# Sliding attention: probability-value products of both heads of a pair in one step, even and odd head in turn

## The chip, the core and the metric

The kernel runs on one core of a Trainium2 chip. The metric is the device time of one execution in microseconds (us). Its engines are TensorE (PE, with its weight loads shown apart as PEld), VectorE (DVE), ScalarE (ACT), GpSimd (POOL) and SyncE (SP); each works through its own program in order, and they wait for each other on semaphores.

## What is computed

One layer of a hybrid decoder, over 2048 tokens with a model width of 1024. The change touches the sliding-window attention in its first part:

```python
h = h + W_out [ HGRN2 head group (4 heads) || sliding-window GQA head group (8 q heads) ](RMSNorm(h))
h = h + CrossAttn_4heads(RMSNorm(h), RMSNorm(mem))
h = h + W_down relu(W_up RMSNorm(h))^2

# swa_group: SW_HEADS = 8, SW_KV_HEADS = 2, SW_HEAD_DIM = 64, SW_BLOCK = WINDOW = 128
s = einsum('bnqhgd,bnkhd->bnhgqk', qb, kw) * 64 ** -0.5     # query block n, key blocks n-1 and n
s = where(valid, s, -inf)
m = maximum(max(s), sink);  p = exp(s - m)
denom = sum(p) + exp(sink - m)
o = einsum('bnhgqk,bnkhd->bnqhgd', p / denom, vw)           # the products that the change touches
```

Everything is float32. The queries of heads 0 to 3 share one head of keys and values, and those of heads 4 to 7 the other.

## The kernel before

The program has three parts in a row: the mixer (both head groups and the projections in front of them), the cross attention and the MLP. The mixer works on four blocks of 512 tokens, and every engine runs the same list of steps for a block. `mixer_steps` writes this list (MIX_STEPS); the last block has its own, LAST_STEPS, made from it, in which a first product of the cross attention (`cross_make`, parts 0 to 2) stands in places that the next block's work left empty. Three sources are interleaved by `weave` at places counted (PLACES): `hg`, the work of a recurrent head; `attend`, the attention of one pair of heads; and `panels`, the projections. A projection ("make") comes in three parts: parts 0 and 1 have eight matmuls each (L1560, L1563), part 2 has eight with the weights' low halves (L1570), all 128 rows by 512 columns. A block runs recurrent head 0, then four times a stretch with the attention of pair t = 0 to 3 (heads 2t and 2t+1) and behind it recurrent head t+1 (behind pair 3 the next block follows). Beside pair t the gates of head t+1 are made, and beside recurrent head 3 the next block's normed input is split (`norm_split`: ACT line 1096, DVE line 1314).

A pair of heads has four sub-steps q = 0 to 3, numbered a = 4t + q: q % 2 says whether the even or the odd head, q // 2 which two of the block's four query tiles of 128. Each sub-step goes through these steps:

- scores: PE (L1702) multiplies queries and keys into one of three banks of PSUM; DVE (L1502) adds mask and scale and takes the extreme of each row; ACT (L1244, L1248) takes the exponentials.
- scale: DVE adds the denominator, inverts it and multiplies the probabilities by it (L1514, L1516, and twice L1519).
- turn: PE transposes the four tiles of 128 by 128 (L1713) into the one bank TURN, and ACT (L1256) copies this bank to pT[a % 2]. PE waits for the copy of a-1 before it writes the bank; ACT waits for the products of a-2 before it writes pT[a % 2].
- pv: PE multiplies (L1725): four matmuls in float32, of which each stands as two records with their weight loads in the trace. The weights are a tile of values with 64 columns, and the products fill rows 0 to 63 of the bank OUT for the even head, rows 64 to 127 for the odd one.

After the fourth pv ACT copies OUT (L1262, step att_out). Then `hg_transpose` follows: PE transposes values (L1612) and decayed keys kend (L1617), and ACT copies both (L1211, and L1214 into ktok), which the products of L1625 (`hg_delta`) need. The scores of a recurrent head (L1642) come in steps of two halves: seven products into rows 0 to 63 of a bank, then seven into rows 64 to 127; the seventh of either half reads hq. The ends of kend and qdec are copied by ACT (L1192, L1193) and scaled by DVE (L1404, L1406) in the step `spans_end`. The output gate (`out_gate`) goes from ACT (L1199) to DVE (L1411) and back (L1202, L1204). A projection's result is taken by ACT (`take`; for queries L1148 and L1149, two activations of 128 by 512).

`attend` yields a group of steps for each n = 0 to 6, and `weave` counts these groups. On PE the steps from the second transposition of pair 1 on read turn, pv, part 2 of a make, turn, pv, turn, pv, pv, and the transpositions of the next recurrent head.

Of the kernel before, what the change touches and what calls it, by code (L numbers as in the profile page):

```python
# [26 lines left out]
P = 128  # L27
# [7 lines left out]
QT = TB // P  # L35
# [7 lines left out]
SW_D = 64  # L43
# [110 lines left out]
def mixer_steps():  # L154


    def rotated(n):
        return [[("sw_norm", n)], [("sw_root", n)], [("sw_rotate", n)]]

    def hg(h, beside):  # L160


        norm, root, rotate = rotated(beside)
        gates = [[("gate_start", h + 1)], [("gate_forget", h + 1)]]
        out = [[("out_gate", h)], [("out_gate_end", h)]]
        yield [("hg_transpose", h)]
        yield [("hg_scores", h, 0)]
        yield [("hg_scores", h, 1)]
        yield [("hg_delta", h)]
        yield norm  # L170
        yield [("hg_state", h)]
        yield [("hg_scores", h, 2)]
        yield root
        yield [("hg_o", h, 0)]
        yield from [out[0]] if h == 0 else [gates[0]] if h + 1 < HEADS else []
        yield [("hg_scores", h, 3)]
        yield [("hg_o", h, 1)]
        yield rotate
        yield from [out[1]] if h == 0 else [gates[0]] if h + 1 == HEADS else []
        yield [("hg_o", h, 2)]  # L180
        yield gates[1] if h else gates[0]
        yield [("hg_o", h, 3)]
        yield [("hg_square", h)]
        yield from [gates[1]] if h == 0 else []

    def hg_tail(h):
        return [[("hg_total", h)], [("hg_end", h)]]

    def attend(t):
        yield []  # L190
        for n in range(QT + 3):
            if n < QT:
                yield [("scores", t * QT + n)]
            if 0 <= n - 1 < QT:
                yield [("scale", t * QT + n - 1)] + [("turn", t * QT + n - 2)] * (n > 1)
            if n == QT + 1:
                yield [("turn", t * QT + n - 2)]
            if n >= 3:
                yield [("pv", t * QT + n - 3)]
        yield [("att_out", t)]  # L200

    def with_out_gate(steps, h):
        steps = list(steps)
        last = steps.index([("turn", h * QT - 1)])
        return steps[:last + 1] + [[("out_gate", h)]] + steps[last + 1:] + [[("out_gate_end", h)]]

    def each(kind):
        return [[(kind, k)] for k in range(KT)]

    yield from weave(hg(0, 0), panels(("sw_v", 0), ("sw_q", 0), ("hg_f", 1)), PLACES["head 0"])  # L210
    yield from weave([[("sw_values",)]] + hg_tail(0) + [[("sw_keys",)]] + rotated(1),
                     panels(("hg_q", 1)), PLACES["keys"])
    for h in range(1, HEADS + 1):
        attention = weave(attend(h - 1), hg_tail(h - 1) if h > 1 else [], PLACES["tail"])
        attention = weave(attention, panels(("hg_v", h), ("hg_g", h), ("sw_q", h) if h < NEXT else ("sw_k", h)), PLACES["pair"])
        attention = weave(attention, gates(h)[2:], PLACES["gates"])
        if h < HEADS:
            attention = with_out_gate(attention, h)
        yield from weave(attention, [[("norm_root", 0)]] if h == 2 else [], PLACES["root"])
        if h + 1 < HEADS:  # L220
            head = weave(hg(h, h + 1), panels(("hg_f", h + 1), ("hg_q", h + 1)), PLACES["head"])
            if h == 1:
                yield from weave(head, each("norm_square"), PLACES["squares"])
            else:
                yield from weave(head, each("norm_apply"), PLACES["apply"])
        elif h < HEADS:
            yield from weave(hg(h, h + 1), each("norm_split") + list(panels(("hg_f", NEXT), ("hg_q", NEXT))), PLACES["head 3"])
# [530 lines left out]
def mixer(nc, block, sems, sh, xT, w_mix, rope_d, y_d, w_cross, lows_d):  # L758
# [13 lines left out]
    OUT = bank[5]  # L772
# [3 lines left out]
    with ExitStack() as ctx:  # L776
# [49 lines left out]
        vsw = sb("vsw", [P, 1 + QT, P])  # L826
        s_sb = sb("s_sb", [P, 3, 2, 2 * P])
        pT = sb("pT", [P, 2, TB])
# [81 lines left out]
        a_pt = signal("probabilities_copied", NA)  # L910
        a_o = signal("attention_output_ready", NA)
# [618 lines left out]
        def _(pe):  # L1530
# [65 lines left out]
            def turn(blk, steps):  # L1596
                for step in steps:
# [70 lines left out]
                    elif kind == "sw_norm":  # L1668
                        n = step[1]
                        pe.wait_ge(copied.sem, copied.at(blk, panel_at("sw_q", n - 1) if n else panel_at("sw_k", 0)))  # L1670
                        if n == 0:
                            total(blk, step, c("ones64"), hsq[:, n % 2, :])
                        else:
                            tile_totals(blk, step, hsq[:, n % 2, :])
                    elif kind == "sw_rotate":
                        n = step[1]
                        if n == 1:
                            pe.wait_ge(k_ok1.sem, k_ok1.at(blk, 0))
                        else:
                            pe.wait_ge(st_ok.sem, st_ok.at(blk, max(n, 1) * (NCH + 1) - 1))  # L1680
                        if n == 0:
                            pe.wait_ge(s_tn.sem, s_tn.at(blk, 0))
                        else:
                            pe.wait_ge(copied.sem, copied.at(blk, panel_at("sw_q", n - 1)))
                        pe.matmul(ROT[:], rotq[:] if n else c("rot"), tn[:, n % 2, :], start=True, stop=True).then_inc(s_rot.sem, 1)
                    elif kind == "sw_keys":
                        pe.wait_ge(s_qk.sem, s_qk.at(blk, 0))
                        pe.wait_ge(v_ok.sem, v_ok.at(blk, 0))
                        pe.matmul(TURN[:], c("dup0"), tcos[:], start=True, stop=True).then_inc(k_dup0.sem, 1)
                        pe.matmul(ROT[:], c("dup1"), tcos[:], start=True, stop=True).then_inc(k_dup1.sem, 1)  # L1690
                    elif kind == "scores":
                        a = step[1]
                        t, q = ATT[a]
                        if q == 0:

                            pe.wait_ge(h_pr.sem, h_pr.at(blk, (t + 1) * NCH // 2 - 1))
                            pe.wait_ge(s_qk.sem, s_qk.at(blk, 1 + t))
                        if q >= 3:
                            pe.wait_ge(a_s.sem, a_s.at(blk, a - 3))
                        for i in range(2):  # L1700
                            tq = q // 2 * 2 + i
                            last = pe.matmul(SCORE[a % 3][:, i * 2 * P:(i + 1) * 2 * P],  # L1702
                                             qk[:, t % 2, tq * P:(tq + 1) * P],
                                             kpad[:, t // 2 * 2 + q % 2, tq * P:(tq + 2) * P], start=True, stop=True)
                        last.then_inc(a_sc.sem, 1)
                    elif kind == "turn":
                        a = step[1]
                        pe.wait_ge(a_pn.sem, a_pn.at(blk, a))
                        if ATT[a][1]:
                            pe.wait_ge(a_pt.sem, a_pt.at(blk, a - 1))  # L1710
                        for kt in range(2):
                            for i in range(2):
                                last = pe.transpose(TURN[:, (2 * kt + i) * P:(2 * kt + i + 1) * P],  # L1713
                                                    s_sb[:, a % 3, i, kt * P:(kt + 1) * P], c("ident"))
                        last.then_inc(a_tr.sem, 1)
                    elif kind == "pv":
                        a = step[1]
                        t, q = ATT[a]
                        if q == 0:
                            pe.wait_ge(h_y.sem, h_y.at(blk, t))  # L1720
                        pe.wait_ge(a_pt.sem, a_pt.at(blk, a))
                        for i in range(2):
                            tq = q // 2 * 2 + i
                            for kt in range(2):
                                last = pe.matmul(OUT[q % 2 * SW_D:(q % 2 + 1) * SW_D, tq * P:(tq + 1) * P],  # L1725
                                                 vsw[:, tq + kt, t // 2 * SW_D:(t // 2 + 1) * SW_D],
                                                 pT[:, a % 2, (2 * kt + i) * P:(2 * kt + i + 1) * P],
                                                 start=kt == 0, stop=kt == 1)
                        last.then_inc(a_o.sem, 1)

            pe.wait_ge(s_xhi, KT)
            pe.wait_ge(s_xln, 4 + KT)
# [1606 lines left out]
```

## Time and profile before

| | us |
|---|---|
| median of 3 runs | 2718.79 |
| lowest, highest | 2718.01, 2720.99 |
| span of the profiled execution | 2717.5 |
| mixer in it, about | 70 to 1012 |
| PE busy in the mixer | 907.6 of 942 |

In the profile a group of instructions is named by its line, its engine, and the tiles that it writes and reads. A matmul's record goes on until its result is out, so records of one step overlap: how fast PE goes is read from the starts, not from the durations. The timeline shows consecutive instructions of a line merged, with the start of the first, the time to the end of the last, and their number.

### The profile page before, as it was taken

The page shows a single profiled execution, that of the slowest core. Times are in us where ns is not written, and L with a number is a line of the kernel's source. Part 1 is how long each engine was busy: PE and PEld are TensorE (multiplying, and loading weights), DVE is VectorE, ACT ScalarE, POOL GpSimd, SP SyncE. Part 2 cuts the span into 40 slices and gives each one's busy share as a digit, 9 for nine tenths or more (in the row PEclk, how much of TensorE's full clock was granted, in tenths as well). Part 3 has the DMA queues.
Part 4 walks back from the last instruction along what each step waited for, and adds up shares of the span by engine and source line. Part 5 has one row for each costly group of instructions (what it writes and reads, how often), then busy time and mean ns, then how long its engine had stood idle before and what let it go on. Part 6 is the DMA issues. An engine that isn't in the chain of part 4 may idle for free.

```text
span 2717.5 us, 39324 instructions
## 1 busy us (share of the span) xinstructions
PE 2635.4 (97%) x13654; PEld 2160.8 (80%) x13654; DVE 1730.3 (64%) x3010; ACT 1146.5 (42%) x2179; POOL 895.6 (33%) x1018
## 2 busy tenths in 40 slices
PE   7999999999999999999999899999999999999999
PEld 5778778777877878777787788888888888888887
DVE  6677566756755665656657486787667354556665
ACT  4455454545544454654565322252223223322231
POOL 1332200000000017436534576747667222222223
PEclk9999999999999999999999999999999999999999
DMA  4422422243243234226315234423333963445664
GB/s 179 140 102 88 171 96 94 94 166 109 86 169 105 86 126 184 70 97 252 116 55 190 85 129 151 138 99 124 105 132 124 328 184 105 134 135 149 202 183 150
DMA packets 184509, 369.17 MB, mean 136 GB/s; under 512 B 13168, under 2 KB 79088, under 8 KB 181616
## 3 DMA queue, kind: packets, MB, share of 16 engines
q1 hardware_dynamic: 179152, 357.08, 39.1%
q10 hardware_dynamic: 5152, 9.51, 1.0%
q8 instruction: 110, 1.80, 0.3%
q14 instruction: 95, 0.78, 0.1%
HBM read 286.71 MB, written 79.82 MB: 135 GB/s over the span
## 4 chain that ended last, share of the span: by engine, by line
PE 76%; DVE 9%; issue 5%; ACT 4%; POOL 3%; DMA 2%; ACTq 0%; DVEq 0%; SPq 0%; POOLq 0%
PE bank L3255 7%; PE bank L3253 7%; PE bank L3257 7%; PE bank L1570 5%; PE bank L3233 5%; PE bank L1560 5%; PE bank L3229 5%; PE bank L3230 5%; PE bank L1563 5%; PE bank L1642 3%; PE bank L2183 2%; PE bank L2178 2%; PE bank L2179 2%; PE bank L1725 2%; PE bank L1702 2%
## 5 line engine op out<-in xcount | busy, mean ns | idle before, releaser
L478 POOL TENSOR_TENSOR wlo<-raw,whi 128x256 fp32r<-128x256 f32 x372 | 320.5, 894 | 1151.5 <-ACT whi L1162 667.5
L1560 PE MATMUL bank<-hi,whi 128*128 128x512 f32 x704 | 296.3, 421 | 2.1 <-ACT whi L1158 1.9
L1563 PE MATMUL bank<-lo,whi 128*128 128x512 f32 x704 | 278.0, 395 | 5.9 <-DVE lo L1314 5.9
L3257 PE MATMUL bank<-hi,wlo 128*128 128x512 f32 x896 | 275.8, 389 | 0.0
L3253 PE MATMUL bank<-hi,whi 128*128 128x512 f32 x896 | 275.8, 389 | 0.0
L3255 PE MATMUL bank<-lo,whi 128*128 128x512 f32 x896 | 275.8, 389 | 0.0
L3045 DVE TENSOR_TENSOR lo<-h,hi 128x1024 fp32r<-128x1024 f32 x80 | 124.6, 1557 | 172.8 <-ACT hi L2809 172.8
L2740 POOL TENSOR_TENSOR wlo<-h,whi 128x256 fp32r<-128x256 f32 x160 | 128.0, 824 | 298.0 <-ACT whi L2801 298.0
L2178 PE MATMUL bank<-hi,whi 128*128 128x512 f32 x504 | 208.6, 414 | 10.0 <-DVE h L2071 5.9
L2179 PE MATMUL bank<-lo,whi 128*128 128x512 f32 x504 | 198.3, 393 | 0.0
L3253 PEld LDWEIGHTS bank<-hi,whi 128*128 128x128 f32 x896 | 168.2, 188 | 34.9
L3257 PEld LDWEIGHTS bank<-hi,wlo 128*128 128x128 f32 x896 | 168.2, 188 | 34.9
L3255 PEld LDWEIGHTS bank<-lo,whi 128*128 128x128 f32 x896 | 168.2, 188 | 34.9
L2722 POOL TENSOR_TENSOR wlo<-raw,whi 128x256 fp32r<-128x256 f32 x166 | 150.2, 931 | 122.7 <-ACT whi L2750 120.3
L1570 PE MATMUL bank<-hi,wlo 128*128 128x512 f32 x704 | 189.4, 411 | 0.0
L2801 ACT ACTIVATE whi<-h 128x512 fp32r<-128x512 f32 x80 | 50.6, 632 | 289.1 <-PE bank L3257 271.6
L1563 PEld LDWEIGHTS bank<-lo,whi 128*128 128x128 f32 x704 | 133.8, 190 | 38.4 <-DVE lo L1314 8.5
L2722 POOL TENSOR_TENSOR m_xlo<-raw,m_xhi 128x256 fp32r<-128x256 f32 x174 | 164.1, 976 | 0.0
L1560 PEld LDWEIGHTS bank<-hi,whi 128*128 128x128 f32 x704 | 133.7, 190 | 34.5 <-issue 7.1
L1570 PEld LDWEIGHTS bank<-hi,wlo 128*128 128x128 f32 x704 | 130.2, 189 | 35.0 <-issue 9.6
L2750 ACT ACTIVATE whi<-raw 128x512 fp32r<-128x512 f32 x87 | 54.5, 628 | 226.3 <-DMA raw<-w_mlp 182.7
L3229 PE MATMUL bank<-hi,whi 128*128 128x512 f32 x348 | 136.0, 391 | 1.9 <-issue 1.1
(395 smaller groups left out, 5935.7 us busy)
## 6 DMA issues: line engine op xcount, KB each, us to landing
h<-hidden_scratch SPq DMA_DIRECT2D x96, 512.0 KB, 4.3
raw<-w_mix SPq DMA_DIRECT2D x88, 512.0 KB, 3.6
raw<-w_cross SPq DMA_DIRECT2D x64, 512.0 KB, 3.3
raw<-w_mlp SPq DMA_DIRECT2D x64, 512.0 KB, 4.7
wlo<-mixer_lows_scratch SPq DMA_DIRECT2D x60, 512.0 KB, 3.5
hidden_scratch<-hT SPq DMA_DIRECT2D x116, 256.0 KB, 2.1
h<-w_mlp SPq DMA_DIRECT2D x112, 256.0 KB, 3.0
mixer_lows_scratch<-wlo SPq DMA_DIRECT2D x22, 512.0 KB, 2.9
```

What stands on the lines that cost most here:

```text
L478: last = pool.tensor_tensor(wlo[:, i, cols], raw[:, i, cols], whi[:, i, cols].bitcast(F32), ALU.subtract)
L1560: pe.matmul(out, w, hi[:, k, :], start=k == 0, stop=False)
L1563: pe.matmul(out, w, lo[:, k, :], start=False, stop=False)
L1570: last = pe.matmul(out, wlo[:, i % 2, k * P:(k + 1) * P], hi[:, k, :], start=False, stop=k == KT - 1)
L2178: pe.matmul(out, w, hi[b][:, k, :], start=k == 0, stop=False)
L2179: pe.matmul(out, w, lo[b][:, k, :], start=False, stop=False)
L2722: last = pool.tensor_tensor(lo_tile[:, cols], source(half, n, w)[:, cols], hi_tile[:, cols].bitcast(F32), ALU.subtract)
L3229: pe.matmul(acc, hi_tile[:, cols], parts(half, m, k)[0], start=k == 0, stop=False)
L3230: pe.matmul(acc, hi_tile[:, cols], parts(half, m, k)[1], start=False, stop=False)
L3253: pe.matmul(down_bank(i)[:], wh[:, cols], xh[:, i % 2, :], start=K == 0, stop=False)
L3255: pe.matmul(down_bank(i)[:], wh[:, cols], xl[:, i % 2, :], start=False, stop=False)
L3257: last = pe.matmul(down_bank(i)[:], wl[:, cols], xh[:, i % 2, :], start=False, stop=K == KD - 1)
```

## The change

`attend` yields a pv step at n = 4 and n = 6 only, for the sub-steps (0, 1) and (2, 3) together. On PE this step waits for the copy of the second of them and then issues eight matmuls: for each of the two query tiles and each of the two key tiles first the even head's, then the odd head's. The last product of either head increments the semaphore a_o, so that its counts stay as they were. Buffers, copies and the other engines' waits are as before; since two groups fewer are yielded per pair, what `weave` puts at later places moves against the attention's steps.

```diff
@@ attend @@
-            if n >= 3:
-                yield [("pv", t * QT + n - 3)]
+            if n >= 3 and n % 2 == 0:
+                yield [("pv", t * QT + n - 4)]
@@ mixer, PE @@
-                        pe.wait_ge(a_pt.sem, a_pt.at(blk, a))
-                        for i in range(2):
-                            tq = q // 2 * 2 + i
+                        pe.wait_ge(a_pt.sem, a_pt.at(blk, a + 1))
+                        for tq in (q, q + 1):
                             for kt in range(2):
-                                last = pe.matmul(OUT[q % 2 * SW_D:(q % 2 + 1) * SW_D, tq * P:(tq + 1) * P],
-                                                 vsw[:, tq + kt, t // 2 * SW_D:(t // 2 + 1) * SW_D],
-                                                 pT[:, a % 2, (2 * kt + i) * P:(2 * kt + i + 1) * P],
-                                                 start=kt == 0, stop=kt == 1)
-                        last.then_inc(a_o.sem, 1)
+                                for odd in range(2):
+                                    last = pe.matmul(OUT[odd * SW_D:(odd + 1) * SW_D, tq * P:(tq + 1) * P],
+                                                     vsw[:, tq + kt, t // 2 * SW_D:(t // 2 + 1) * SW_D],
+                                                     pT[:, odd, (2 * kt + tq - q) * P:(2 * kt + tq - q + 1) * P],
+                                                     start=kt == 0, stop=kt == 1)
+                                    if tq == q + 1 and kt:
+                                        last.then_inc(a_o.sem, 1)
```

What PE does around the attention of pair 1 in the first block, from its second transposition on (bank6 is TURN, bank5 OUT, con the identity, vsw the values; pairs 2 and 3 read alike). Before:

```order
L1713 MATMUL bank6<-con,s_sb 128x128 x4
L1725 MATMUL bank5<-pT,vsw 64x128 x4
L1570 MATMUL bank1<-hi,wlo 128x512 x8
L1713 MATMUL bank6<-con,s_sb 128x128 x4
L1725 MATMUL bank5<-pT,vsw 64x128 x4
L1713 MATMUL bank6<-con,s_sb 128x128 x4
L1725 MATMUL bank5<-pT,vsw 64x128 x8
L1612 MATMUL bank6<-con,vT 128x128 x4
```

And in the changed kernel, the same engine and place:

```order
L1713 MATMUL bank6<-con,s_sb 128x128 x8
L1570 MATMUL bank1<-hi,wlo 128x512 x8
L1725 MATMUL bank5<-pT,vsw 64x128 x8
L1713 MATMUL bank6<-con,s_sb 128x128 x4
L1725 MATMUL bank5<-pT,vsw 64x128 x8
L1612 MATMUL bank6<-con,vT 128x128 x4
```

The second and third transposition now stand behind each other, the first products have moved behind part 2 of the make, and the fourth transposition stands right behind them. For pair 0 a part of a make stands both after the third transposition and after the fourth.

ACT at the same place, as a difference (pT is the copy of TURN, tn and hsq the taken queries):

```order
 L1248 ACTIVATE stat<-stat,sink 128x2
-L1256 ACTIVATE pT<-bank6 128x512
+L1256 ACTIVATE pT<-bank6 128x512 x2
 L1188 REGISTER_ALU
 L1192 ACTIVATE kend<-h 128x8x32
 L1193 ACTIVATE qdec<-h 128x8x32
-L1256 ACTIVATE pT<-bank6 128x512
-L1122 REGISTER_ALU
-L1145 REGISTER_ALU
-L1148 ACTIVATE tn<-bank1 128x512
-L1149 ACTIVATE hsq<-bank1 128x512
 L1256 ACTIVATE pT<-bank6 128x512
```

The third copy has moved ahead of L1192 and L1193, and the take of the queries behind the fourth copy and the output gate. For pair 0 L1192 and L1193 themselves come behind the output gate. DVE's third and fourth scale also stand behind each other; the scale that the third transposition needs has kept its place.

PE at pair 3 in the last block, where the cross attention's product (L1583) stands beside the attention. Before:

```order
L1713 MATMUL bank6<-con,s_sb 128x128 x4
L1583 MATMUL bank0<-hi,wlo 128x512 x8
L1725 MATMUL bank5<-pT,vsw 64x128 x4
L1713 MATMUL bank6<-con,s_sb 128x128 x4
L1725 MATMUL bank5<-pT,vsw 64x128 x4
```

In the changed kernel:

```order
L1702 MATMUL bank2<-kpad,qk 128x256 x2
L1713 MATMUL bank6<-con,s_sb 128x128 x8
L1583 MATMUL bank0<-hi,wlo 128x512 x8
L1725 MATMUL bank5<-pT,vsw 64x128 x8
L1713 MATMUL bank6<-con,s_sb 128x128 x4
```

The third transposition has moved ahead of the eight matmuls of L1583.

## Rows read from the trace of the kernel before

**Rows 1.** The page: its head, and the busy time of each engine

```profile
span 2717.5 us, 39324 instructions
PE 2635.4 (97%) x13654; PEld 2160.8 (80%) x13654; DVE 1730.3 (64%) x3010; ACT 1146.5 (42%) x2179; POOL 895.6 (33%) x1018
```

**Rows 2.** Stretches: the mixer; busy us of PE, PEld, DVE, ACT, POOL, then clock

```profile
70.00:1012.00 942.00, 907.60 (x6022) 745.89 (x6022) 609.75 (x1588) 474.34 (x1028) 81.57 (x106) 0.99 0.34 115
```

**Rows 3.** Groups by form: the products; number, busy us, mean ns

```profile
L1725 PE MATMUL bank<-pT,vsw 128*64 128x128 f32 x512 | 64.3, 279 | 0.0
```

**Rows 4.** Timeline, PE, second block, pair 2: start us, us, instructions, [idle before]

```profile
493.01 0.60 PE L1713 MATMUL bank<-con,s_sb 128*128 128x128 f32 x4
493.54 1.09 PE L1725 MATMUL bank<-pT,vsw 128*64 128x128 f32 x8
494.56 2.12 PE L1570 MATMUL bank<-hi,wlo 128*128 128x512 f32 x8
496.52 0.60 PE L1713 MATMUL bank<-con,s_sb 128*128 128x128 f32 x4
...
498.07 0.66 PE L1713 MATMUL bank<-con,s_sb 128*128 128x128 f32 x4
498.65 1.84 PE L1725 MATMUL bank<-pT,vsw 128*64 128x128 f32 x16
500.43 0.66 PE L1612 MATMUL bank<-con,vT 128*128 128x128 f32 x4
```

**Rows 5.** Timeline, recurrent head's scores behind it: both halves of one step

```profile
502.25 0.22 PE L1642 MATMUL bank<-h 128*64 128x64 f32 x1
502.25 0.22 PE L1642 MATMUL bank<-hq,h 128*64 128x64 f32 x1
```

**Rows 6.** Timeline, first block, pair 2: PE waits for a copy

```profile
254.82 0.58 ACT L1256 ACTIVATE pT<-bank 128x512 f32<-128x512 f32 x1
255.54 0.63 PE L1713 MATMUL bank<-con,s_sb 128*128 128x128 f32 x4 [0.86 <-ACT pT L1256]
```

**Rows 7.** Timeline, pair 2 of rows 4 on DVE, ACT and PE

```profile
493.93 0.62 DVE L1519 TENSOR_SCALAR s_sb<-s_sb,stat 128x256 f32<-128x256 f32 x2
498.76 0.60 ACT L1256 ACTIVATE pT<-bank 128x512 f32<-128x512 f32 x1
501.11 0.63 ACT L1204 ACTIVATE w<-w 128x512 f32<-128x512 f32 x1
503.33 0.60 ACT L1214 ACTIVATE ktok<-bank 128x512 f32<-128x512 f32 x1
504.32 0.94 PE L1625 MATMUL bank<-vtok,ktok 128*128 128x128 f32 x6
```

**Rows 8.** Timeline, first block: scales of pairs 1 and 2

```profile
201.80 0.60 PE L1713 MATMUL bank<-con,s_sb 128*128 128x128 f32 x4
203.25 0.62 DVE L1519 TENSOR_SCALAR s_sb<-s_sb,stat 128x256 f32<-128x256 f32 x2
258.21 0.62 DVE L1519 TENSOR_SCALAR s_sb<-s_sb,stat 128x256 f32<-128x256 f32 x2
```

**Rows 9.** Timeline, third block, pair 0: PE and ACT

```profile
621.12 0.60 PE L1713 MATMUL bank<-con,s_sb 128*128 128x128 f32 x4
626.06 0.41 ACT L1193 ACTIVATE qdec<-h 128x256 f32<-128x256 f32 x1
630.43 0.65 PE L1612 MATMUL bank<-con,vT 128*128 128x128 f32 x4
```

**Rows 10.** Timeline, PE, last block, pair 3: third transposition, start of the cross attention

```profile
1004.59 0.63 PE L1713 MATMUL bank<-con,s_sb 128*128 128x128 f32 x4 [0.81 <-ACT pT L1256]
...
1008.53 0.50 PE L2178 MATMUL bank<-hi,whi 128*128 128x512 f32 x1
```

**Rows 11.** Stretches around a low clock: columns as in rows 2

```profile
513.70:517.10 3.40, 1.44 (x7) 0.77 (x8) 3.34 (x7) 0.00 (x0) 0.00 (x0) 1.00 0.00 0
517.10:520.50 3.40, 3.40 (x30) 3.09 (x29) 1.13 (x3) 0.00 (x0) 0.00 (x0) 0.51 0.02 5
```

## The prediction, made before the changed kernel ran

> **What bounds the kernel now.** I read the page's busy times first: TensorE (PE) is busy for 97% of the span, and no other engine for more than 64% [rows 1]. Then the table by stretches: the mixer, where the whole change lies, is no exception, with 907.6 of 942 us [rows 2]. The reader is to see that here a microsecond in which PE issues nothing is a microsecond of the span, and one saved is saved, unless a wait takes it back. Third, the group of the products: 512 records, 64.3 us [rows 3]. Fourth, the timeline of one pair [rows 4]: turn, products, make, turn, products, turn, products twice. There is no idle time ahead of any of them that a wait would explain; each step starts as soon as the one before it is issued. All other engines' work around it is hidden behind PE. So I look for two things: what PE issues less, and which copies lose their cover.
>
> **What it saves.** (1) *Halves side by side.* Eight records of one head take 1.09 from first start to last end, and 1.02 to the next step (493.54 to 494.56). Two heads one behind the other, 16 records, take only 1.84 [rows 4]. One behind the other at some 0.11 a record they would take 1.09 + 0.87 = 1.96; the odd head began 1.84 - 1.09 = 0.75 after the first start, before the even one's last record had. The recurrent scores show it more plainly: the seventh product of the first half ("hq,h") and a product of the second half start at the same 502.25 [rows 5]. So the two column halves of the array work side by side, each at its own rate. Merged and alternating, 16 records should take one head's time plus about 0.05: 1.07 to the next step, in place of 1.02 + 1.02, or of the last two's 1.78. (2) *Changes of shape.* A transposition costs 0.53 to the next start ahead of products, 0.59 between two of them, and the products' 1.02 holds some 0.2 in which nothing starts; between equal shapes the four transpositions should take 0.44. There are three excursions per pair now, two after, so some 0.25 less.
>
> If nothing waited, pair 1, 2 or 3 would take, from the second transposition on: 0.44 + 0.44 + 1.82 (the make's eight at 0.227, its 1.96 less the change of shape) + 0.09 + 1.07 + 0.59 + 1.07 = 5.5, against 7.42 now (493.01 to 500.43) [rows 4]. That is 1.9 less, over 16 pairs 30 us.
>
> **What it uncovers.** A copy of TURN costs PE this: records end, 0.04 later ACT starts, 0.60, and 0.14 more until PE starts, as where PE waits now (copy ends 255.40, PE starts 255.54) [rows 6]. From a last end that is 0.78. Such copies lay behind products or a make. Three now don't, in pairs 1 to 3 (T is the second transposition's start):
> - *Third transposition, T2.* It stands right behind the second. It needs the second's copy (0.60 + 0.78 = T + 1.38) and its own scaled probabilities. DVE, whose order up to there is unchanged, ends these at 494.55, T + 1.54 [rows 7], so T2 = T + 1.68. PE was ready at T + 0.44.
> - *Fourth transposition.* T2, then 0.44 + 1.82 + 0.09: products at T2 + 2.35. The third copy writes the half of pT that the even head's products read, so it waits for their end: start T2 + 2.35 + 1.09 + 0.04 = 3.48, end 4.08, fourth transposition T2 + 4.22. Before, the first products had long been done. ACT is in order, so L1192 and L1193 wait behind this copy; they still end before the fourth.
> - *Last products.* Transposition's end 4.85, copy to 5.49, products T2 + 5.63, next step T2 + 6.70.
>
> Sum: 1.68 + 6.70 = 8.38 in place of 7.42, **+0.96**. This holds for eight pairs (blocks 2 to 4, pairs 1 to 3, less the last). In the first block DVE is slower: the scale ends at T + 2.07 for pair 1 (203.87 less 201.80) [rows 8], and at T + 3.29 for pair 2 (258.83 less 255.54) [rows 6, 8]. By the same sum these cost 2.21 + 6.70 - 7.42 = +1.5 and 3.43 + 6.70 - 7.42 = +2.7; the third I take between them, +2.1.
>
> Pair 0 has a make's part behind both the third and the fourth transposition, so only two waits. T2 = T + 1.38 (the scale is done); next transposition T2 + 4.22; then 0.47 + 1.82 + 0.09 and 1.07: T2 + 7.67, T + 9.05, against 9.31 now (621.12 to 630.43) [rows 9]. Saved: 0.26. But ACT now copies kend behind the output gate. The fourth copy ends at T2 + 5.49, the gate's last step 2.38 after the copy, as now (499.36 to 501.74) [rows 7], and L1192 and L1193 (0.41 each, a little overlapped) end at about T2 + 8.5. PE wants kend at T2 + 8.16 and gets it at 8.63: +0.47. Net +0.2 each.
>
> Last pair of the last block: now the third transposition starts at 1004.59, because it waits for a copy, and the cross product and the first products fill the time ahead of it [rows 10]. Afterwards both stand behind it. From 1004.59 on 6.70 gives 1011.3, against 1008.53: **+2.8**.
>
> Behind pair 2 no make stands ahead of L1625, which needs ktok. Now the fourth copy ends at 499.36 and ktok at 503.93, T + 10.92; PE comes at 504.32, T + 11.31 [rows 7]. Afterwards the take (two activations, 1.08) lies between as well: T + 1.68 + 5.49 + 4.57 + 1.08 = T + 12.82, and PE can start at 12.96, having been ready at 11.31 + 0.96 = 12.27. That is +0.7; ACT's splits of the next input are behind it and PE waits for them a little later, which adds ACT's remaining delay, 1.90 - 1.65 = 0.25. **+0.9**, four times.
>
> **Sum.** Pair 0: 4 x 0.2 = 0.8. First block: 1.5 + 2.7 + 2.1 = 6.3. Eight pairs: 7.7. Last: 2.8. Behind pair 2: 3.6. In all +21.2. Against the profiled span 2717.5 that is 2738.7 [rows 1]; the median of the runs stands 1.3 above this span, so **2740**. Unknown sizes: the restart of an idle PE (0.14, or next to nothing where its queue is filled) over some 43 waits, -5 at most; the alternating pair's rate, where a start each 0.06 in place of 0.055 gives +2. The increments stay as many as before (one per head and pair of tiles), so they cost nothing more.
>
> **Rivals.**
> *Serial halves.* If strict alternation lets the second head's load wait for the first head's matmul, a merged step takes 1.02 + 0.87 = 1.89, 0.82 more, and both of a pair are on the path: 32 x 0.82 = 26, so 2766. Rows 4 and 5 speak against it, but they show two long runs that meet, not records in turn. The Trainium skill (TensorE: Matmul & The Clock Gate, What overlaps and what doesn't, under Packing small matmuls) says that a weight load overlaps a matmul in flight only if it goes to another row group. Both heads use all 128 rows, so by that rule this rival is what happens; the records that start together disagree with it.
> *Low clock.* Behind a stretch in which PE was busy for 1.44 of 3.40 us the granted clock fell to 0.51, near 1.2 in place of 2.4 GHz, for 3.40 us [rows 11]; that costs some 1.7. The new place, from the end of the first products to the end of the last, has about 1.75 busy in 3.2: a little denser. Were it to happen in half of the 12 such places: +10, 2750.
> *Given back.* PE idles 34 us in the mixer as it is [rows 2]. If those waits were for work that doesn't depend on PE, a late PE would find it done, and most of the 21 would vanish: 2720. Against: what I see of them (copies, scales, splits) is released by PE's own results.
> *Faster.* PE runs through without the waits: -30, so 2688. This needs the copies to be covered after all. It decides at a mean added wait of 30/43 = 0.7 a place; my sum has 51/43 = 1.2, and even ACT's copy alone is 0.60 of it. What speaks for it is the size of what is saved, and that the third transposition's wait is the largest and rests on DVE's time.
>
> **How the numbers follow.** My forecast 0.61 (its own range 2728 to 2751); serial 0.10; low clock 0.13; given back 0.09; faster 0.07. The range takes the forecast, the low clock and part of "given back": 2722 to 2756. A measurement of this kernel can tell about 0.2%, some 5.4 us, from no change. Faster by more than that: 0.07; within: 0.10, "given back" and a sliver of the forecast; slower: 0.83.
>
> **What would show it.** Timeline of a pair after: 16 records in about 1.14 (right) or 1.96 (serial). Ahead of L1713 three kinds of idle that weren't there: about 1.2 for the third transposition, released by DVE's scale; 0.6 to 0.9 for the fourth, released by ACT's copy; and 0.6 to 0.9 ahead of the last products. PE's busy time in L1725 falls from 64.3 to 35 to 40, while L1713 waits some 25 to 30 us. L1617 waits in pair 0, L1625 behind pair 2. L1713 to L2178 in the last block grows by about 3. I am wrong if the starts of a pair show no idle, or if the mixer's other waits shrink by as much as these grow.

## The result

| | us |
|---|---|
| before, median of 4 runs | 2718.53 |
| changed kernel, median of 4 runs | 2742.14 (2741.11 to 2743.41) |
| ratio to before, 95% interval | 1.0082 (1.0068 to 1.0095) |
| forecast, range | 2740 (2722 to 2756) |
| span of the profiled execution, before and after | 2717.5, 2741.6 |

The changed kernel is 0.8% slower. The 95% interval of the ratio lies clear of 1. Below are the page's head and busy times, and the mixer's row of the table by stretches (busy us of PE, PEld, DVE, ACT and POOL, then the clock, the DMA share and GB/s). They answer to [rows 1] and [rows 2]:

```profile
span 2741.6 us, 39324 instructions
PE 2615.6 (95%) x13654; PEld 2136.3 (78%) x13654; DVE 1730.1 (63%) x3010; ACT 1146.0 (42%) x2179; POOL 893.5 (33%) x1018
70.00:1035.00 965.00, 887.42 (x6028) 721.76 (x6027) 610.02 (x1590) 475.04 (x1030) 82.14 (x106) 0.98 0.33 113
```

The mixer ends some 24 us later, and PE is busy in it for 20 us less: 887.4 against 907.6. Outside the mixer nothing moved by more than 0.3 us. The groups by form, as in [rows 3], say both things at once:

```profile
L1713 PE MATMUL bank<-con,s_sb 128*128 128x128 f32 x256 | 40.1, 280 | 35.2 <-ACT pT L1256 21.3 <-DVE s_sb L1519 13.9
L1725 PE MATMUL bank<-pT,vsw 128*64 128x128 f32 x512 | 35.5, 282 | 8.3 <-ACT pT L1256 8.3
```

The products (L1725) take 35.5 us instead of 64.3. But PE now idles 35.2 us ahead of the transpositions, for copies and for DVE's scales, and 8.3 us ahead of the products; before it was 2.0 and none. The timeline of PE in the second block, pair 2, which answers to [rows 4], shows where:

```profile
505.91 0.60 PE L1713 MATMUL bank<-con,s_sb 128*128 128x128 f32 x4
507.50 0.66 PE L1713 MATMUL bank<-con,s_sb 128*128 128x128 f32 x4 [0.99 <-DVE s_sb L1519]
507.91 2.09 PE L1570 MATMUL bank<-hi,wlo 128*128 128x512 f32 x8
509.93 1.09 PE L1725 MATMUL bank<-pT,vsw 128*64 128x128 f32 x16
511.86 0.63 PE L1713 MATMUL bank<-con,s_sb 128*128 128x128 f32 x4 [0.83 <-ACT pT L1256]
513.17 1.09 PE L1725 MATMUL bank<-pT,vsw 128*64 128x128 f32 x16 [0.69 <-ACT pT L1256]
514.20 0.66 PE L1612 MATMUL bank<-con,vT 128*128 128x128 f32 x4
```

Sixteen records take 1.09 us, as long as eight did: the two heads run side by side. From the second transposition to L1612 it is nevertheless 8.29 us instead of 7.42. Three waits, 0.99, 0.83 and 0.69, stand where there were none. On ACT, the third and the fourth copy of the same pair:

```profile
511.12 0.60 ACT L1256 ACTIVATE pT<-bank 128x512 f32<-128x512 f32 x1 [3.88 <-PE bank L1725]
512.52 0.60 ACT L1256 ACTIVATE pT<-bank 128x512 f32<-128x512 f32 x1 [0.20 <-PE bank L1713]
```

The third copy waits 3.88 us, and its releaser is no longer the transposition but the products (L1725), which must have read pT[0] first.

Pair by pair, from the second transposition to the next work, the difference between the two traces is: pair 0 -0.16 to -0.18 in every block; pairs 1 to 3 of blocks 2 to 4, without the last, +0.86 to +0.89; first block +0.98, +5.12 and +2.01; last pair +4.29.

### The profile page after: what moved, and what is told of

The parts are those of the page before. It is cut to its first block, busy times and chain, and to the rows that moved or that the text cites. A ratio compares the mean times of both kernels' runs of the same rounds, so it can differ in the third digit from the quotient of the medians.

```text
span 2741.6 us, 39324 instructions
## 1 busy us (share of the span) xinstructions
PE 2615.6 (95%) x13654; PEld 2136.3 (78%) x13654; DVE 1730.1 (63%) x3010; ACT 1146.0 (42%) x2179; POOL 893.5 (33%) x1018
## 4 chain that ended last, share of the span: by engine, by line
PE 70%; DVE 10%; issue 7%; ACT 5%; POOL 5%; DMA 1%; ACTq 0%; DVEq 0%; POOLq 0%; SPq 0%
PE bank L3256 7%; PE bank L3254 7%; PE bank L3258 7%; PE bank L1570 5%; PE bank L1560 4%; PE bank L1563 4%; PE bank L3234 4%; PE bank L3230 4%; PE bank L3231 4%; PE bank L1642 3%; PE bank L2184 2%; PE bank L2179 2%; PE bank L2180 2%; POOL wlo L2723 2%; POOL m_xlo L2723 2%
```

## The experiments

Every run is compared with the kernel before, run beside it on the same chip: its medians there were 2719.3 (one head then the other, places kept, third copy apart, last pair mended), 2718.48 (the third copy with places kept, the last pair with both, the rearrangement) and 2719.39 (the last two). The changed kernel itself was measured in another session, and medians of different groups can't be compared to better than about 1 us. Below, T is again the start of a pair's second transposition, and "the end" the start of the work behind its last products.

### One head, then the other

```diff
-                        for tq in (q, q + 1):
-                            for kt in range(2):
-                                for odd in range(2):
+                        for odd in range(2):
+                            for tq in (q, q + 1):
+                                for kt in range(2):
```

> The changed kernel with one thing undone: a merged step issues the even head's four matmuls first and then the odd head's four. Waits, semaphores and the order of all steps stay as in the changed kernel. In its trace the two heads' records start 7 ns apart and 16 records take 1.09 us. My theory (column halves side by side; the first merged step of a pair is followed by PE's wait for a copy that hangs on the even head only): the odd half of the first merged step is issued inside that wait and costs nothing, the last merged step of a pair takes about 1.78 instead of 1.02 to the next step, so 16 x 0.75 = +12: 2754. Rival A, the alternation is worth nothing, because two halves that follow each other overlap in the queue anyway: 2742. Rival B, both merged steps are on the path: +24, 2766.

Measured: 2747.91, ratio 1.0098 (1.0081 to 1.0114). Second block, pair 2, on PE:

```profile
509.62 1.58 PE L1725 MATMUL bank<-pT,vsw 128*64 128x128 f32 x16
511.55 0.63 PE L1713 MATMUL bank<-con,s_sb 128*128 128x128 f32 x4 [0.34 <-ACT pT L1256]
512.86 1.58 PE L1725 MATMUL bank<-pT,vsw 128*64 128x128 f32 x16 [0.69 <-ACT pT L1256]
```

The place is as the theory has it: the first merged step grows by 0.49 and the wait behind it shrinks by 0.49 (0.83 to 0.34), while the last step's 0.49 lands on the path. The size is not: 0.49, not 0.75. Even without alternation PE starts the second head while the first still runs. The kernel before issues the same records in the same order, but with a wait for a semaphore between the heads, and takes 1.84 [rows 4]; my 0.75 came from there. That the wait makes this difference is not shown. 16 x 0.49 = 7.8; the medians differ by 5.8. Both rivals fall: the last step grows in every pair, and only the last step costs anything.

### The makes' places kept

```diff
-            if n >= 3 and n % 2 == 0:
-                yield [("pv", t * QT + n - 4)]
+            if n >= 3:
+                yield [("pv", t * QT + n - 4)] * (n % 2 == 0)
```

> The changed kernel, but attend still yields its groups for the products at n = 3 and n = 5, empty. So weave puts the makes where they stood before: a make's part stands again between the second and the third transposition, and the merged products stand right behind the third (n = 4) and the fourth (n = 6). Theory: most of the loss is the third transposition's uncovered wait and what hangs on the shift (kend behind pair 0, the take ahead of ktok behind pair 2), not the merging. Per pair 1 to 3: 0.44 + 1.82 + 0.44 + 0.09, fourth transposition 1.93 after that, 2.34 to the end: 7.06 against 8.29; pair 0: 8.04 against 9.13 and no wait for kend (-0.5); behind pair 2 -0.9; first block's slow scales gone, -9; the last pair as in the changed kernel. In all about -29: 2713. Rival, the waits come from the merged step's copies and not from the shift: above 2735.

Measured: 2718.57, ratio 0.9997 (0.9987 to 1.0006): the whole loss is gone, and nothing is gained. Second block, pair 2, on PE:

```profile
493.48 0.60 PE L1713 MATMUL bank<-con,s_sb 128*128 128x128 f32 x4
493.84 2.10 PE L1570 MATMUL bank<-hi,wlo 128*128 128x512 f32 x8
495.78 0.60 PE L1713 MATMUL bank<-con,s_sb 128*128 128x128 f32 x4
496.31 1.09 PE L1725 MATMUL bank<-pT,vsw 128*64 128x128 f32 x16
498.24 0.63 PE L1713 MATMUL bank<-con,s_sb 128*128 128x128 f32 x4 [0.83 <-ACT pT L1256]
499.61 1.09 PE L1725 MATMUL bank<-pT,vsw 128*64 128x128 f32 x16 [0.75 <-ACT pT L1256]
500.64 0.66 PE L1612 MATMUL bank<-con,vT 128*128 128x128 f32 x4
```

The make is back between the second and the third transposition and covers copy and scale; of the three waits the first is gone. T to the end is 7.16 (expected 7.06), pair 0's 8.11 (8.04). So two things take the change's gain in a pair: the shift of the makes, and the two copies that the merging itself uncovers. The expected 29 were 24, of which the 16 pairs of the traces show 20.7; the last pair is still at +4.04 against the kernel before. The rival, above 2735, falls.

### The third copy apart

```diff
-                        act.wait_ge(a_o.sem, a_o.at(blk, a - 2))
+                        if a % QT != 2:
+                            act.wait_ge(a_o.sem, a_o.at(blk, a - 2))
...
-                        act.activation(pT[:, a % 2, :], TURN[:], ACT.Copy).then_inc(a_pt.sem, 1)
+                        act.activation(ktok[:] if a % QT == 2 else pT[:, a % 2, :], TURN[:], ACT.Copy).then_inc(a_pt.sem, 1)
```

The products read the same tile; ktok is free from L1625 of one recurrent head to L1214 of the next.

> The changed kernel with one thing more: ACT copies the third transposition of a pair (a % 4 == 2) into ktok, which is idle during the attention, in place of pT[0], and doesn't wait for the even head's first products any more. Everything else is unchanged. Theory: the fourth transposition no longer waits for a copy; it follows the first merged products after 1.0 instead of 1.93 us. That is 16 x 0.9 = -14.5: 2728. Rival, the wait only moves: the fourth transposition's own probabilities or ACT's other work end just as late, so that nothing or less than 4 us is gained.

Measured: 2737.39, ratio 1.0062 (1.0045 to 1.0078), 4.8 less than the changed kernel instead of 14.5: as a time, a miss. Second block, pair 2, on PE:

```profile
503.19 1.09 PE L1726 MATMUL bank<-pT,vsw 128*64 128x128 f32 x16
504.21 0.66 PE L1714 MATMUL bank<-con,s_sb 128*128 128x128 f32 x4
```

The fourth transposition follows after 1.02 instead of 1.93, without a wait, and T to the end is 7.42 instead of 8.29: 0.87 less in this pair and in every undisturbed one like it. So the mechanism stands, and neither DVE nor the fourth scale is late next. The 16 pairs together take 12.1 us less than in the changed kernel, but the stretches between them take 5.4 more. Mean clock of this trace, and below it that of the changed kernel's:

```profile
core 0: 2735.7 us, clock 0.989
core 0: 2741.6 us, clock 0.991
```

The largest part lies in the last block, from the end of pair 2 to the last pair, first here and then in the changed kernel (columns as in [rows 2]):

```profile
979.77:1013.43 33.66, 29.66 (x218) 25.70 (x217) 23.34 (x55) 17.25 (x42) 3.29 (x4) 0.80 0.25 102
990.27:1020.35 30.08, 25.78 (x218) 22.70 (x217) 23.48 (x56) 17.26 (x42) 3.29 (x4) 0.89 0.28 114
```

As many records, 218, take 3.6 us longer, at a mean clock of 0.80 in place of 0.89. By estimate the low clock accounts for 0.20 x 33.66 - 0.11 x 30.08 = 3.4 of them. All four runs of this variant have a mean clock of 0.989, and those of the changed kernel 0.991 to 0.993, so it belongs to the variant and not to one execution; why the clock falls more often in it is not shown. The time alone would have told me that the theory was two thirds wrong; the pairs say that it was right.

### The last pair mended

```diff
-                      (("cross_make", 1), ("scores", _first + 3)), (("cross_make", 2), ("pv", _first)), (("cross_second",), ("pv", _first))):
+                      (("cross_make", 1), ("scores", _first + 3)), (("cross_make", 2), ("turn", _first + 2)), (("cross_second",), ("pv", _first))):
```

> The changed kernel with the order of the last pair of the last block mended: the third part of the cross attention's first product stands again ahead of the third transposition, which waits there for a copy. Theory: the last pair gives back what it lost, 2 to 4 us (it took 4.3 more in the changed kernel than before, 1.5 of this at a low clock): 2738 to 2740. Rival: the product waits for nothing and is simply late, so that its place doesn't matter: 2742.

Measured: 2741.63, ratio 1.0074 (1.0057 to 1.0091). Nothing can be told from this time: the four runs lie between 2737.58 and 2748.68, and the profiled one is the slowest. Its trace has the last pair at +3.06, against +4.29, with its products at the low clock (1.95 us for 16 records that take 1.09 otherwise). Inconclusive; the same edit is tried again below.

### Places kept and third copy apart

> The two edits together: empty groups keep the makes in their places, and the third copy goes into ktok. With the places kept alone a pair 1 to 3 took 7.14 us from its second transposition on, with the fourth transposition 1.9 after the first merged products; with the third copy apart this distance was 1.0. Theory (two waits that add up, each with its own cause): the fourth transposition at T + 3.85 instead of 4.74, the end at T + 6.25, 0.9 less for each of 12 pairs; pair 0 unchanged, because a make covers its copy: 2718.6 - 11 = 2708. Rival, ACT or DVE become the bound once PE runs through (fourth scale or third copy late): less than 4 of the 11 arrive.

Measured: 2708.75, ratio 0.9960 (0.9944 to 0.9975). T to the end is 6.22 in pairs 1 to 3 (expected 6.25), pair 0 unchanged at 8.11. The two waits add up, each with its own cause; the rival falls.

### And the last pair

> The kernel with both edits, and in the last block the third part of the cross attention's product stands again ahead of the third transposition of the last pair. In the changed kernel this edit alone took 1.2 us from the last pair, although its runs as a whole didn't show it (2741.6 against 2742.1). Theory: the 1 to 3 us of the last pair are real, but the time of single runs moves by as much with the places at which the clock happens to be low: 2705 to 2707. Rival: nothing, 2708.

Measured: 2703.34, ratio 0.9942 (0.9926 to 0.9957), 5.4 less. The last pair on PE without the edit:

```profile
986.45 0.63 PE L1714 MATMUL bank<-con,s_sb 128*128 128x128 f32 x4 [0.37 <-ACT pT L1257]
990.75 1.09 PE L1714 MATMUL bank<-con,s_sb 128*128 128x128 f32 x4 [3.68 <-ACT pT L1257]
991.49 3.22 PE L1584 MATMUL bank<-hi,wlo 128*128 128x512 f32 x8
```

and with it:

```profile
985.57 0.63 PE L1714 MATMUL bank<-con,s_sb 128*128 128x128 f32 x4 [0.37 <-ACT pT L1257]
985.95 2.09 PE L1584 MATMUL bank<-hi,wlo 128*128 128x512 f32 x8
989.87 0.63 PE L1714 MATMUL bank<-con,s_sb 128*128 128x128 f32 x4 [1.83 <-ACT pT L1257]
```

The wait goes from 3.68 to 1.83, and the eight matmuls from 3.22 to 2.09, since the clock is no longer low. The pair takes 3.3 us less, and every other pair the same to 0.02. So the price of this place, with the low clock behind it, is real; in the run of this edit alone it was hidden. The other 2 us of the medians' 5.4 lie outside the pairs, and their cause is not shown.

### Every copy covered, by rearrangement

> A rearrangement, in which every copy has cover: in pairs 1 to 3 each transposition stands one place earlier (the first ahead of a make's part 0, the second ahead of part 1), the merged products behind part 1, then the third transposition, part 2 and the fourth; in pairs 0 and 1 the next make's part 0 stands between the fourth transposition and the last products; the take stands behind the fourth copy; the third copy goes into ktok. Theory: pairs 0 and 1 save the whole 1.9 of merging against the kernel before, pairs 2 and 3 save 1.1 (the last products still wait 0.8), ktok comes 1.0 late behind pair 2: 4 x (1.9 + 1.9 + 1.1 + 1.1 - 1.0) = 20 less than before: 2699. Rival: PE is the bound only on paper here, and the scales of DVE or ACT's order take back what is saved: 2710 or more.

Measured: 2714.16, ratio 0.9983 (0.9974 to 0.9992); a miss. PE's largest wait in the mixer (engine, tile, line, releaser; us in total, times, longest), and below it one of these waits, ahead of the first products of pair 1 in the second block:

```profile
PE bank L1759 <- ACT pT L1290: 16.0, 20, 1.8
...
439.02 1.09 PE L1759 MATMUL bank<-pT,vsw 128*64 128x128 f32 x16 [0.85 <-ACT pT L1290]
```

I had put the second transposition behind the last scores. ACT works in order, so its copy stood behind the exponentials of these scores, which wait for DVE, and the first products, ahead of which no wait was expected, idled 0.85. That is 12 pairs x 0.85 = 10 of the 15 us missed. The profiled execution had a mean clock of 0.992, and that of the kernel before 0.994, which by estimate is 0.002 x 2714 = 5 us; that this is the rest is not shown.

### The last products covered too

```diff
+def last_products_later(steps):
+    for t in range(2):
+        make = next(s for s in steps[steps.index(("pv", t * QT + 2)):] if s[0] == "make")
+        if t == 0:
+            make = next(s for s in reversed(steps[:steps.index(("turn", 3))]) if s[0] == "make")
+        steps.remove(make)
+        steps.insert(steps.index(("pv", t * QT + 2)), make)
+    return steps
...
-MIX_STEPS = [s for steps in mixer_steps() for s in steps]
+MIX_STEPS = last_products_later([s for steps in mixer_steps() for s in steps])
```

> The best kernel so far (places kept, third copy apart, last pair mended: 2703.3) with cover for the last products of pairs 0 and 1, which are 8 of the 16 waits of 0.69 us that are left ahead of merged products: in pair 0 the make's part 2 moves from ahead of the fourth transposition to behind it, in pair 1 the next projection's part 0 moves ahead of the last products. Theory: PE is the bound and every covered copy is worth its wait, 8 x 0.69 = -5.5: 2698. Rival: the make moved in pair 0 uncovers the third copy again (fourth transposition right behind the first products), which costs up to half of it in four pairs: 2700 to 2701.

Measured: 2699.70, ratio 0.9934 (0.9920 to 0.9947). This is the lowest median of all, but its interval overlaps that of the kernel that it builds on (0.9926 to 0.9957). The wait in question, first in the kernel with the last pair mended, then here:

```profile
PE bank L1726 <- ACT pT L1257: 11.0, 16, 0.7
```

```profile
PE bank L1737 <- ACT pT L1268: 5.5, 8, 0.7
```

Half of it is gone, 5.5 us; the medians differ by 3.6, between theory and rival. The traces decide it: behind the first products of pair 0 the fourth transposition starts without a wait (1.03 us after them in the second block), so the rival's cost isn't there. In the first block it waits 0.91 for DVE's scale instead, which the theory did not have.

### One head, then the other, where nothing waits behind

> The best kernel so far (2703.3) with a merged step's products not in turn: four of the even head, then four of the odd one. In the changed kernel this undoing cost 0.49 per pair, in the last products alone, since the first ones lay inside a wait. Here the first ones have no wait behind them. Theory: what the alternation is worth in itself is 0.49 for each merged step, so 32 x 0.49 = +16: 2719, which is the time of the kernel before. Rival: as in the changed kernel only the last products count, +8: 2711.

Measured: 2715.54, ratio 0.9985 (0.9976 to 0.9995), 12.2 more than 2703.34: a time halfway between theory (+16) and rival (+8). T to the end is 7.19 instead of 6.22, so both merged steps of a pair now cost their 0.49 (0.97 together, 15.5 over 16 pairs), and by the pairs the rival falls. The medians show less than the pairs. The ten runs lie between 2712.24 and 2723.00 with mean clocks of 0.996 to 0.991, the faster the higher the clock, so the low clock is the likely reason; this is argued and not shown.

## Why the prediction was right

**The bound.** Right. PE's waits for other work in the mixer did not shrink by as much as the new ones grew. This row reads the same before and after:

```profile
PE bank L1536 <- ACT sqsum L1220: 7.0, 4, 1.8
```

Three others moved by over 1 us; the first row of each couple is from before, the second from the changed kernel:

```profile
PE bank L1563 <- DVE lo L1314: 5.9, 6, 1.1
PE bank L1563 <- DVE lo L1314: 4.5, 5, 1.1
PE bank L1655 <- DVE st L1430: 5.4, 4, 3.0
PE bank L1655 <- DVE st L1430: 6.6, 4, 3.4
PE bank L1685 <- ACT kpad L1236: 4.5, 4, 1.1
PE bank L1685 <- ACT kpad L1236: 3.3, 3, 1.1
```

Together they give back 1.4 us, while the waits of L1713 and L1725 grew by 41.5. So "given back" was wrong, as argued, and "faster" with it.

**Side by side.** Right, and better than taken: 16 records in 1.09, where I had allowed 0.05 more. The rival of serial halves, which needed 1.89, is refuted by the same row. The Trainium skill (TensorE: Matmul & The Clock Gate, What overlaps and what doesn't) says that weight loads overlap a matmul in flight only in another row group. Both heads use all rows and run side by side all the same, so this trace disagrees, and the measurement decides.

**What is uncovered.** All three waits came in their places, with the releasers named. The sizes:

| term | forecast | measured |
|---|---|---|
| third transposition | T + 1.68 | T + 1.59 |
| fourth, after the third | 4.22 | 4.36 |
| to the end | 2.48 | 2.34 |
| pairs 1 to 3, blocks 2 to 4 | +0.96 | +0.86 to +0.89 |
| pair 0 | -0.26 | -0.16 to -0.18 |
| first block, pairs 1, 2, 3 | 1.5, 2.7, 2.1 | 0.98, 5.12, 2.01 |
| last pair | +2.8 | +4.29 |

The first is 0.09 shorter because PE starts 0.05 after DVE ends (507.45, 507.50), not 0.14. The 0.14 holds ahead of the fourth transposition (the copy ends at 511.72, PE starts at 511.86), but ahead of the last products it is 0.05 again, behind a copy too (513.12, 513.17). The second and third row are off by 0.14 each way and cancel: together they are the 6.70 that was forecast, which is luck. In the first block pair 1 came in low because DVE had the scale ready at T + 1.65 and not T + 2.07: L1382 ahead of it took 0.54 us, and 0.95 in the trace before, from which I read. Pair 2 is far off, and this is the low clock, which I had as a rival and not as a part of the sum:

```profile
257.00:260.60 3.60, 1.33 (x8) 0.66 (x6) 3.56 (x9) 3.18 (x9) 3.01 (x4) 1.00 0.73 229
260.60:267.40 6.80, 5.51 (x22) 4.27 (x24) 2.69 (x12) 0.00 (x0) 0.00 (x0) 0.50 0.45 157
```

PE, busy for 1.33 of 3.60 us because its transposition waited for the scale, was granted 0.50 of the clock, 1.2 GHz, for the next 6.8 us, and the make took 3.76 instead of 2.1. That makes 5.12 out of 2.7. The last pair met the same (its product took 3.61): 4.29 out of 2.8.

**Behind the pairs.** Both indirect costs are there. In pair 0 L1617 waits for qdec's copy:

```profile
643.39 0.66 PE L1612 MATMUL bank<-con,vT 128*128 128x128 f32 x4
644.37 0.63 PE L1617 MATMUL bank<-con,kend 128*128 128x128 f32 x4 [0.32 <-ACT qdec L1193]
```

0.98 from step to step in place of 0.49, as the forecast's 0.47 more; behind pair 2 L1625 waits for ktok:

```profile
518.80 1.46 PE L1625 MATMUL bank<-vtok,ktok 128*128 128x128 f32 x11 [0.63 <-ACT ktok L1214]
```

The forecast had 0.7, and 0.9 with what follows; the traces lie 0.86 to 0.97 apart there in the three blocks where the clock doesn't disturb the comparison.

**The sum.** Terms without the clock: pair 0 4 x 0.3, first block 1.0 + 2.7 + 2.0, eight pairs 7.0, last 2.8, behind pair 2 3.7, in all 20.4, against 21.2 forecast. The clock adds 2.4 in the first block and 1.5 in the last pair: 24.3, and the traces' ends of the mixer's attention lie 24.35 apart (1008.53 and 1032.88). That they meet so closely is luck. Between the pairs the low clock fell in other places in the two traces: the changed one loses 1.7 and 1.6 us behind pair 0 of the first two blocks, and regains 1.5 behind pair 2 of the second and 1.0 behind pair 3 of both, which nearly cancels. The low clock should have stood in the forecast with some 2 to 4 us instead of a rival that takes the whole or nothing. The terms that were there were 0.8 too high and the missing one was 3.9, so the forecast of 21.2 came out 3.1 below the traces' 24.35, and 2740 came out 2.1 below the median.

## What to carry to other kernels

Where one engine is the bound and its steps hide other engines' copies, merging two steps removes a cover along with the work: count, for each copy in the loop, what still stands between its producer and its consumer. An order written as places in a list moves when the list gets shorter; here an empty entry in place of the removed one gave back the whole 0.8%. And when a buffer is free only after a merged step, give the next copy another one: with both, the last pair's order mended and a make ahead of the last products, the same merging ended 0.66% ahead of the kernel before.

## What the runs showed of the hardware

- Matmuls that fill different halves of the output rows ran side by side at full rate in strict alternation: 16 float32 records of 128 columns in 1.09 us, exactly the time of 8.
- They overlapped without alternation too: with four matmuls of one head and then four of the other, 16 records took 1.58, where one behind the other would by estimate be 1.96. PE started the second head's about 0.5 us after the first's, well before these were done. With a wait between the heads, as in the kernel before, it was 1.84.
- TensorE's clock fell from 2.4 to 1.2 GHz behind a wait inside the mixer: PE was busy for 1.33 of 3.60 us, and 6.8 us at 0.50 of the clock followed. A wait of 2.69 us stood in a pair that took 5.12 more.
- Such stretches move the time of this kernel by several us between variants (mean clock 0.989 to 0.994 in the profiled executions). The last pair's order, worth 3.3 us in its pair, showed as 5.4 in the medians; tried alone it was worth 1.2 in its pair and showed as 0.5. Such an edit is better read pair by pair.
